# The 83 matmuls of ident and ones (166 in the trace) are taken out of a hybrid encoder layer

## What is computed

```
mod = silu(c) @ w_ada + b_ada            # 9 vectors of 1024: shift, scale, gate for three branches
h = rms_norm(x, g) * (1 + scale) + shift
x += 0.5 * gate1 * (silu(h @ w1) * (h @ w3)) @ w2        # FFN 1, inner width 2816
h = rms_norm(x) modulated;  z = h @ w_in                 # 3584 columns
y = concat(hgrn2(z), rg_lru(z)) @ w_out                  # the mixer
x += gate2 * y
x += 0.5 * gate3 * swiglu(h)                             # FFN 2
return rms_norm(x, final_norm)
```

## Time and profile before

| | us |
|---|---|
| time, median of 3 runs | 1123.32 |
| lowest and highest of them | 1123.31 and 1124.42 |
| the profiled execution: span, first to last instruction | 1122.3 |
| PE matmul busy | 1066.8 (95% of the span), 4902 instructions |
| PE weight loads busy | 873.7 (78%) |
| VectorE busy | 606.9 (54%) |
| ScalarE busy | 404.6 (36%) |
| GpSimd busy | 163.9 (15%) |
| mean granted TensorE clock | 0.981 of full speed |

### The profile page before, as it was taken

How to read it: one execution, slowest core, us unless ns; L and a number is a source line. 1 busy time by engine, 2 the same in 40 slices (tenths; PEclk the granted TensorE clock), 3 DMA queues, 4 the chain that set the end, 5 groups by cost and what they waited for, 6 DMA issues and landing times.

```text
span 1122.3 us, 13691 instructions
## 1 busy us (share of the span) xinstructions
PE 1066.8 (95%) x4902; PEld 873.7 (78%) x4902; DVE 606.9 (54%) x700; ACT 404.6 (36%) x516; POOL 163.9 (15%) x149
## 2 busy tenths in 40 slices
PE   3899999999999999998998888999999999999997
PEld 3788888888888888786776767778888888888885
DVE  5877677633342326659899899553333333322324
ACT  3242222222311223575865665343232222222211
POOL 2211111000000101016382533010000000000100
PEclk9799999999999999998999899999999999999999
DMA  8678788622222223221111111213322223222222
GB/s 300 230 246 278 262 264 262 203 91 97 94 94 93 94 94 139 78 82 49 56 57 57 51 43 39 76 57 108 98 93 93 93 95 105 98 94 94 93 94 75
DMA packets 37393, 132.41 MB, mean 118 GB/s; under 512 B 4080, under 2 KB 4336, under 8 KB 37232
## 3 DMA queue, kind: packets, MB, share of 16 engines
q1 hardware_dynamic: 28992, 100.83, 26.7%
q0 software_dynamic: 8368, 31.13, 8.2%
HBM read 129.85 MB, written 2.10 MB: 118 GB/s over the span
## 4 chain that ended last, share of the span: by engine, by line
PE 83%; DVE 10%; issue 3%; DMA 2%; ACT 2%; SPq 0%; DVEq 0%; ACTq 0%
PE psum L1127 25%; PE psum L1129 24%; PE psum L1128 24%; PE psum L1362 2%; PE psum L1376 1%; DVE qk L976 1%; DMA ada<-wada 1%; PE psum L1332 1%; DVE qk L975 1%; PE psum L1164 1%; DVE acc L697 1%; DMA raw<-wu 1%; DVE wlo L673 1%; PE psum L1233 1%; PE psum L1303 1%
## 5 line engine op out<-in xcount | busy, mean ns | idle before, releaser
L673 DVE TENSOR_TENSOR wlo<-raw,whi 128x1024 fp32r<-128x1024 f32 x166 | 209.3, 1261 | 340.9 <-ACT whi L358 340.7
L358 ACT ACTIVATE whi<-raw 128x1024 fp32r<-128x1024 f32 x168 | 177.9, 1059 | 563.6 <-PE psum L1129 549.0
L1127 PE MATMUL psum<-hhi,whi 128*128 128x512 f32 x896 | 359.6, 401 | 10.5 <-DVE sg L927 5.4
L1128 PE MATMUL psum<-hlo,whi 128*128 128x512 f32 x896 | 351.9, 393 | 0.0
L1129 PE MATMUL psum<-hhi,wlo 128*128 128x512 f32 x896 | 351.6, 392 | 0.0
L1127 PEld LDWEIGHTS psum<-hhi,whi 128*128 128x128 f32 x896 | 170.3, 190 | 50.9 <-DVE wlo L673 7.7
L1129 PEld LDWEIGHTS psum<-hhi,wlo 128*128 128x128 f32 x896 | 170.1, 190 | 36.3
L1128 PEld LDWEIGHTS psum<-hlo,whi 128*128 128x128 f32 x896 | 170.4, 190 | 35.4 <-issue 1.9
L1127 PE MATMUL psum<-ghi,whi 128*128 (+1 forms) x352 | 138.5, 394 | 0.0
L1129 PE MATMUL psum<-ghi,wlo 128*128 (+1 forms) x352 | 138.1, 392 | 0.0
L1128 PE MATMUL psum<-glo,whi 128*128 (+1 forms) x352 | 136.8, 389 | 0.0
(11 more groups left out here) (172 smaller groups left out, 970.7 us busy)
## 6 DMA issues: line engine op xcount, KB each, us to landing
raw<-wu SPq DMA_DIRECT2D x168, 512.0 KB, 3.3
ada<-wada POOLq DMA_DIRECT2D x56, 512.0 KB, 5.0
ada<-wada SPq DMA_DIRECT2D x16, 512.0 KB, 4.7
x<-xt SPq DMA_DIRECT2D x2, 1024.0 KB, 10.2
out<-outt SPq DMA_DIRECT2D x8, 256.0 KB, 2.2
bd<-bd POOLq DMA_DIRECT2D x1, 1024.0 KB, 5.1
dif<-consts POOLq DMA_DIRECT2D x1, 448.0 KB, 6.1
resets<-consts POOLq DMA_DIRECT2D x1, 256.0 KB, 6.9
```

The source lines that it names most:

```text
L358: nc.scalar.activation(whi[:, slot, :], raw[:, slot, :], ACT.Copy).then_inc(hi_done, 1)
L673: nc.vector.tensor_tensor(wlo[:, slot, :], raw[:, slot, :], whi[:, slot, :], ALU.subtract).then_inc(lo_done, 1)
L1127: nc.tensor.matmul(dst, a, rhi, start=start, stop=False)
L1128: nc.tensor.matmul(dst, a, rlo, start=False, stop=False)
```

## The change

`keep_busy` and all its calls are taken out; `norm_turn` loses its parameter b. The order of all other instructions and all waits stay as they are on every engine.

```diff
-            def keep_busy(b, n):
-
-                for _ in range(n):
-                    nc.tensor.matmul(bank[b][:, 0:P], ident[:], ones[:], start=True, stop=True)
-
-            def norm_turn(n, b):
+            def norm_turn(n):
 
                 norm_sums(n, 1)
-                keep_busy(b, 3)
                 norm_sums(n, 2)
-                keep_busy(b, 5)
                 norm_rb(n)
-                if n < 3:
-                    keep_busy(b, 11)
...
             pe.wait_ge(sq_done, 1)
-            keep_busy(4, 11)
             norm_sums(0, 0)
             mod_sum(0)
-            keep_busy(4, 7)
             norm_sums(0, 1)
             norm_sums(0, 2)
-            keep_busy(4, 3)
             norm_rb(0)
-            keep_busy(4, 8)
             mod_sum(1)
-            keep_busy(4, 8)
...
-            norm_turn(1, 5)
+            norm_turn(1)
...
-            norm_turn(2, 2)
+            norm_turn(2)
...
-            norm_turn(3, 5)
+            norm_turn(3)
```

## The result

The changed kernel takes 1128.45 us (median of 11 runs); the kernel before, run beside it, 1124.42 (11 runs, the three shown above among them). The ratio is **1.0033**, 95% interval 1.0023 to 1.0044: 3.7 us slower, interval 2.6 to 4.9. The forecast was +6.0 us in a range of +2.0 to +7.9. The profiled execution has a span of 1126.2 us, 3.9 above the 1122.3 of before.

The account below looks back on a forecast made before the run. PE was taken to bound the kernel (83% of the chain of waits). A 0, B 3.38, C 1.82 and D 0.83 gave +6.0 us on 1123.3, so 1129.3 us; range +2.0 to +7.9 (1125.3 to 1131.2).

Parts of the forecast that it names:

- rb at the lower clock: Broadcast of the inverse root at B, C and D: slower at the halved clock, +0.88 us each.
- B: Place between FFN 1 and the mixer; its terms together +3.38 us.
- C: Place between the mixer and FFN 2; its terms together +1.82 us.
- D: The final norm; no wide work follows, its terms together +0.83 us.
- The time of the idents: Removed matmuls no longer delay the next one: -0.15 us at B, -0.05 each at C and D, nothing at A.
- Restart of the mixer: At B: the mixer's first wide matmuls run 5.7 us at the lower clock and pay in full, +2.65 us.
- Restart of FFN 2: At C: first wide matmuls run at the lower clock, partly hidden behind the wait for hlo, +0.99 us.
- A: Place before FFN 1: narrow sums run cold but slack of 1.7 us covers it, 0 us, bounds -0.3 and +0.7.
- Around the span: Whole kernel: median of the runs taken to lie 1.0 us above the profiled span of 1122.3 us.

Follow-up runs that it names:

- behind_rb_only: Kernel before, with only the 11 idents behind rb in each norm turn taken out; ratio 1.0007 (0.9996 to 1.0018).
- warm_start: Kernel before without the start's 37 idents, but 5 put between rb and the last modulation sum and 14 behind it; ratio 0.9979, 2.4 us faster.
- start_only: Kernel before with only the 37 idents of the start taken out, those of the norm turns kept; ratio 0.9983, measured again 0.9973.
- pool_later: Kernel before with all idents, GpSimd's third add of squares waiting also for VectorE's first multiply of the second modulation sum; ratio 0.9991.
- after_again: The changed kernel, all idents out, measured once more against the kernel before for a second profile; ratio 1.0031.
- narrow_turns: Kernel before with every ident of the norm turns writing 1 column and not 128, the start unchanged; ratio 1.0070, +7.9 us.
- turns_only: Kernel before with only the idents of the three norm turns taken out, the 37 of the start kept; ratio 1.0040, +4.5 us.
- rest_of_start: Kernel before with the first 11 idents of the start kept and its other 26 taken out; ratio 0.9992 (0.9981 to 1.0002).

## Why the prediction was right, and where it was off

The forecast had the sign, the range and the cause; the size was 2.3 us too large. Its +6.0 is near the +5.9 and +6.4 that the two profiles show behind the start, but some luck is in that: errors of single terms cancel. By its steps:

- **rb at the lower clock, +0.88 each.** Measured 2.08, 2.07 and 2.07 us against 1.13, 1.13 and 1.12: +0.95 each. The clock was down before rb began at B and C in both profiles of the changed kernel, as was expected from the earlier trace rows. The cold also reached the last of the sums at D (1.15 us for 1.05), hence +1.04 there.
- **The time of the idents, -0.25.** It was 0. B and C take 7.41 to 7.42 us with the 11 idents behind rb and without them (behind_rb_only): the wide matmul starts 0.15 us after its hlo in either case. I took PE's reaction to a semaphore for a wait behind idents.
- **Restart of the mixer, +2.65.** Measured +2.26 and, in the second profile, +2.56, cold for 5.2 and 5.6 us, where I took 5.7. At 0.20 us for every 0.43 that is 2.4 and 2.6, so the mixer's own waits hid next to nothing of it, as assumed.
- **Restart of FFN 2, +0.99.** Measured +0.87 and +0.90, cold for 5.4 and 5.5 us; warm_start shows the same 1.0 at FFN 1. By the rule of the Trainium skill, "TensorE: Matmul & The Clock Gate", section "HAM oscillation — how this bites in real kernels", half the cold time, that would be 2.7 us, an estimate. The rule is near the mixer (2.6 and 2.8 for +2.26 and +2.56), which PE bounds, and does not fit FFN 2, whose PE waits for hlo.
- **A, taken as 0 with bounds -0.3 and +0.7.** This is the term that failed: -1.94 and -2.02 in the two profiles, -1.10 and -2.16 in those of start_only, whose times are 1.9 and 3.0 us shorter and whose spans 1.4 and 1.9. I had looked only at the slack of the cold sums against the arrival of the second weight unit, and taken that arrival as fixed. It is not. And I had not seen that the first hlo takes 2.33 us and ends with GpSimd's wlo.
- **How A came to move.** The first norm sums at 1.2 GHz let ACT's squares and GpSimd's add come 0.7 us later. VectorE's multiply L694 is then through before the add begins, 0.75 us for 1.67 (beside the add it ended 0.55 us after it). The two loads of w_ada that wait for L694 and the addition behind it are issued at 25.78 and 28.11, not 26.85 and 29.05. The loads behind them, the weight units among them, are issued within 0.2 us of before, but land sooner: the two weight units at 37.75 and 40.08 for 38.79 and 42.03. So what moved is the time from issue to landing, 7.5 us for the second unit and not 9.4; the DMA engines moved 316 GB/s between 28 and 32 us after the change and 278 before. With that landing alone GpSimd's second wlo could have begun at 42.0, where the rows of before put the end of its first at the soonest: -1.2 us, an estimate. The other 0.8 is that fin ends 0.75 us sooner: the root is there 0.57 sooner, as no idents stand ahead of its sums, and the last load of w_ada no longer holds fin up. pool_later shows the steps from L694 to the second whi; the division of the -1.9 us rests on the rows of single executions.
- **Around the span.** I had put 1.0 us there, span against a median of three runs. In the record it is 1.6 to 3.0 us for the kernel before and 1.6 or 1.7 for the changed one, whose difference in after_again is 3.8 us by the spans and 3.5 by the times.

## What to carry to other kernels

Work that nobody reads can be worth its place if it keeps TensorE at its upper clock across a gap, and the place decides: 8 idents ahead of rb and 11 behind it gain 4.5 us here (4.9 by the span), 37 more at the start lose 1.9 (3.0 in a second measurement; 1.4 and 1.9 by the span). The filler that held the clock wrote 128 columns; with 1 column it kept PE occupied, the clock fell at two of three places, and the kernel was slower than with none (+7.9 against +4.5). And a transfer's arrival is not a fixed point: before costing a change against it, look at what issued the transfers ahead of it. Last, a variant whose time moves as expected proves a link only if the stage that it speaks of moved: pool_later gained its microsecond elsewhere.

## Hardware behaviour that I had not expected

- PE had been busy since 422.4 without a gap, with matmuls of one column, when the granted clock fell to 0.50 at 425.1, and it stayed there through 22 more in 4.69 us (narrow_turns, at B; at D it did not fall before 1121.4).
- VectorE's first hlo beside GpSimd's wlo took 1.44 to 2.73 us and ended 0.55 us after it in all 13 profiles; alone it takes 0.75.
- The edges of a cold stretch move between executions of the same instructions: rb at C was 2.07 us in the changed kernel and 1.73 in turns_only; in the kernel before the first 22 idents took 5.00 us and the sums behind them were warm (1.05), in rest_of_start they took 4.12 and the sums were cold (1.77), and in narrow_turns, whose start is that of before, no rise of the clock stands before 32.5 and the sums took 1.87.
- The profile's granted clock is not to be trusted before its first change. In the changed kernel it reads 1.00 over the whole start:

```profile
22.50:44.20 21.70, 14.64 (x58) 1.00 0.91 329
```

Yet the 16 narrow matmuls there took 3.57 us, as at 0.50 in the kernel before, and rb 2.08.
